# Latent attention on one core: groups of two heads and two query tiles, scores from row halves and row quarters, turned weights moved by two engines

## The chip, the cores and the metric

The kernel runs on one core of one Trainium2 chip. The metric is the device time of one execution in microseconds. The kernel before takes 4449.14 us in the median of three runs (4448.75 to 4455.67). All data is float32.

## The reference, cut to what matters

The program runs a window attention layer, a latent attention layer and then further layers (retention, stick-breaking, RWKV). Only the latent attention and the gate stage behind it are touched. Per head, with 1280 keys (256 of context, 1024 of the sequence) and 1024 queries:

```
s = (einsum("bqhd,bkhd->bhqk", qn, kn) + einsum("bqhd,bkd->bhqk", qr, kr)) * scale   # 64 deep, and 32 deep
p = softmax(s, axis=-1)
o = einsum("bhqk,bkhd->bqhd", p, v)
y = (o * silu(g)) @ w_out
```

There are 16 heads. The rope part `kr` is the same for all heads.

## The kernel before, in words

`latent_attention` (lines 1232 to 1427) works in units of one head and one query tile of 128 rows: 16 heads by 8 tiles make 128 units. Two neighbouring units of a head make a pair. Nope and rope rows of a head stand on 96 partitions of `qT` and `kT`, so that one float32 matmul computes a score chunk.

For a unit, PE makes the scores in three matmuls of 512, 512 and 256 columns into three banks (L1371). VectorE reads all 1280 at once into `s_sb`, scaled, with the row maximum (L1313), and negates the maximum (L1315). ScalarE takes the exponential in place, with the row sum (L1290). PE turns the ten 128 by 128 blocks of weights (L1389) into three banks; ScalarE moves eight of them to `pT` in two copies of 512 columns (L1301), VectorE two in a copy of 256 (L1329). For a pair of units PE multiplies the values (L1404): the two units go to the two column halves of the array, 64 columns each, so the result is a transposed `o`, which VectorE copies (L1323), PE turns back (L1376) and VectorE normalises into `o` (L1336).

The order on each engine is written out by hand. On PE it is, for unit u: scores of u + 1, one half of the values of an earlier pair, turning of u, and every second unit a turn back. A loop of six rounds runs over passes of two heads each, with a first and a last pass outside it.

SP loads a head with five transfers (L1268 to L1272) into one of two slots, and after the first two heads it prefetches (L161, L172) the gate weights `wg0` and `wg1` (2 MB each) and `wo` (4 MB) and two tiles of columns. `gate_and_project` (L753) then runs product with `wg`, silu, gating, turning and product with `wo`. Its window instance has only `wg0` prefetched and loads `wg1` and `wo` at its start; its latent instance before has all three prefetched.

Of the kernel before, what the change touches and what calls it, by code (L numbers as in the profile page):

```python
# [752 lines left out]
def gate_and_project(nc, core, name, o, tiles, weights, late, columns, gate_rows):  # L753


    with ExitStack() as mem:
# [13 lines left out]
        with nc.Block() as block:  # L770
# [30 lines left out]
            def _(dve):  # L801
                def gates(i):
                    dve.wait_ge(silu_made, i + 1)
                    dve.wait_ge(ogT_made, i)
                    dve.tensor_tensor(og[:, :], silu[:, :], o[:, tiles[i], :], ALU.mult).then_inc(og_made, 1)
# [426 lines left out]
def latent_attention(nc, core, q_dram, qr_dram, k_dram, kr_dram, v_dram, o, prefetch):  # L1232
# [5 lines left out]
    PASSES, UNITS, PAIRS = H // 2, 2 * QT, QT  # L1238
    FRONT_TILES, BACK_TILES = range(0, 4), range(4, 8)
    HALVES = [range(0, KT // 2), range(KT // 2, KT)]  # L1240
    with ExitStack() as mem:
        sb = lambda n, shape: mem.enter_context(nc.sbuf_tensor(f"{name}_{n}", shape, F32))
        qT, kT, v = sb("qT", [B_QK, 2, QT * P]), sb("kT", [B_QK, 2, K]), sb("v", [P, 2, KT, B_V])
        s_sb, pT, oT = sb("s", [P, 2, K]), sb("pT", [P, 3, K]), sb("oT", [P, 2, P])
        smax, total, inverse = sb("smax", [P, 2, 1]), sb("total", [P, 2, 2]), sb("inverse", [P, 2, 2])
        head_in = [nc.alloc_semaphore(f"{name}_head_in{s}") for s in range(2)]
        s_made, s_steps, p_made, pT_made, pT_act, pT_dve, o_made, oT_moved, inverse_made, back_read = (
            nc.alloc_semaphore(f"{name}_{n}") for n in (
                "s_made", "s_steps", "p_made", "pT_made", "pT_act", "pT_dve", "o_made", "oT_moved", "inverse_made", "back_read"))
        s_banks, pT_banks = core.banks(0, 3)[:, 0:K], [core.banks(3 + c) for c in range(3)]  # L1250
        tail_bank, back_bank = pT_banks[2][:, 0:2 * P], pT_banks[2][:, 2 * P:3 * P]
        o_bank = [core.banks(6 + n)[:, 0:P] for n in range(2)]

        def passes(eng, run):
            run(lambda per, k: k, True, False)
            with eng.Fori(0, PASSES - 2) as j:
                run(lambda per, k: j * per + (per + k), False, False)
            run(lambda per, k: (PASSES - 1) * per + k, False, True)

        pT_of = lambda u: (u // 2) % 2 if u % 2 == 0 else 2  # L1260
        with nc.Block() as block:

            @block.sync
            def _(sp):
                values_of = v_dram.rearrange("(t p) n -> p t n", p=P)

                def load(h, s):
                    sp.dma_start(qT[0:B_NOPE, s, :], q_dram[h]).then_inc(head_in[s], 16)  # L1268
                    sp.dma_start(qT[B_NOPE:B_QK, s, :], qr_dram[h]).then_inc(head_in[s], 16)
                    sp.dma_start(kT[0:B_NOPE, s, :], k_dram[h]).then_inc(head_in[s], 16)  # L1270
                    sp.dma_start(kT[B_NOPE:B_QK, s, :], kr_dram).then_inc(head_in[s], 16)
                    sp.dma_start(v[:, s, :, :], values_of[:, :, bass.ds(h * B_V, B_V)] if not isinstance(h, int) else values_of[:, :, h * B_V:(h + 1) * B_V]  # L1272
                                 ).then_inc(head_in[s], 16)

                load(0, 0)
                load(1, 1)
                prefetch(sp)
                with sp.Fori(0, PASSES - 1) as j:
                    for s in range(2):
                        hold(sp, o_made, j * PAIRS + (s + 1) * (PAIRS // 2))  # L1280
                        load(j * 2 + (s + 2), s)

            @block.scalar
            def _(act):
                one_table(act)

                def exp(count, u):
                    act.wait_ge(s_steps, count(UNITS * 2, u * 2 + 2))
# [1726 lines left out]
```

## Time and profile before

| what | before |
|---|---|
| time, median of three runs | 4449.14 us |
| time of the profiled execution | 4446.34 us |
| its span | 4444.3 us |
| mean granted TensorE clock | 0.969 |
| PE busy | 4115.8 us, 93% |
| PE weight loads busy | 2420.0 us, 54% |
| VectorE busy | 1506.5 us, 34% |
| ScalarE busy | 1223.9 us, 28% |
| score matmuls of the latent attention (L1371) | 300.9 us |
| its turning (L1389) | 168.9 us |
| its values (L1404) | 167.8 us |

How to read it: the span is what the profiler sees from first to last instruction. An engine's busy time joins overlapping instructions. A float32 matmul appears as two MATMUL records (two passes), a transpose as one. [...] "Idle before" is the time in which the engine had nothing in progress, with what ended it in brackets. The latent attention lies between 1229 and 1840 us of the span.

### The profile page before, as it was taken

How to read it: one execution, taken by the hardware profiler on the slowest of the kernel's cores; microseconds unless marked ns; L12 is line 12 of the kernel's file. 1: busy time of each engine (PE TensorE's matmuls, PEld its weight loads, DVE VectorE, ACT ScalarE, POOL GpSimd, SP SyncE). 2: the span in 40 equal slices, each digit the busy share in tenths (PEclk: the TensorE clock that was granted, in tenths of full speed). 3: DMA queues.
4: the chain of work that ended last, by engine and by line, in shares of the span. 5: the costliest groups of instructions: out<-in, count | busy, mean ns of one | idle time of the engine just before them, and what ended most of it. 6: DMA issues, size and time to landing. Idle time of an engine off the chain costs nothing. (4 is left out here: it accounts for less than half of the span.)

```text
span 4444.3 us, 69604 instructions
## 1 busy us (share of the span) xinstructions
PE 4115.8 (93%) x29154; PEld 2420.0 (54%) x29154; DVE 1506.5 (34%) x2878; ACT 1223.9 (28%) x2133; POOL 319.9 (7%) x143
## 2 busy tenths in 40 slices
PE   7999999989999999998999998998999968898798
PEld 1446864445466666543554455444444468888343
DVE  0335641122144544211331044012222266656111
ACT  0116750012245555301221045112222222211132
POOL 0000000000000000000000000000000037565000
PEclk9999999989999999999999999998999989999899
DMA  8200020042241111002002002005111121110300
GB/s 276 87 15 23 2 77 19 10 101 77 94 129 33 33 33 33 20 14 99 14 14 95 14 1 95 0 0 189 52 43 47 52 106 46 64 65 27 142 19 19
DMA packets 170633, 253.37 MB, mean 57 GB/s; under 512 B 79446, under 2 KB 97046, under 8 KB 170392
## 3 DMA queue, kind: packets, MB, share of 16 engines
q1 hardware_dynamic: 170398, 249.90, 16.9%
q8 instruction: 189, 3.10, 0.3%
q14 instruction: 46, 0.38, 0.0%
HBM read 187.27 MB, written 62.60 MB: 56 GB/s over the span
## 5 line engine op out<-in xcount | busy, mean ns | idle before, releaser
L237 PE MATMUL psum<-rp_w,rp_mixed 128*128 128x512 f32 x1024 | 448.2, 596 | 6.7 <-issue 3.6
L237 PEld LDWEIGHTS psum<-rp_w,rp_mixed 128*128 128x128 f32 x1024 | 194.3, 191 | 248.4 <-issue 242.2
L1371 PE MATMUL psum<-la_kT,la_qT 96*128 96x512 f32 (+1 forms) x768 | 300.9, 528 | 15.3 <-DMA la_v<-latent_v 13.0
L2323 POOL TENSOR_TENSOR rs_kk<-rs_k,rs_k_k 128x1024 f32<-128x1024 f32 x7 | 16.5, 2364 | 3711.7 <-DVE rs_k L2667 3589.0
L1313 DVE TENSOR_SCALAR_CACHE_REDUCE la_s<-psum 128x1280 f32<-128x1280 f32 x128 | 191.0, 1492 | 238.7 <-PE psum L1371 238.7
L237 PE MATMUL psum<-retention_w,even_hT 128*128 128x512 f32 x544 | 240.2, 603 | 7.8 <-PEq L112 6.3
L237 PE MATMUL psum<-output_wo,pg_oT 128*128 128x512 f32 x512 | 230.8, 610 | 11.5 <-DMA output_wo<-in_even_w_out_dram 5.4
L237 PE MATMUL psum<-output_wg,pg_xT 128*128 128x512 f32 x512 | 227.4, 602 | 7.3 <-ACT pg_xT L1954 7.3
L1301 ACT ACTIVATE la_pT<-psum 128x512 f32<-128x512 f32 x256 | 139.0, 595 | 289.7 <-PE psum L1389 289.7
L1371 PEld LDWEIGHTS psum<-la_kT,la_qT 96*128 96x128 f32 x768 | 137.1, 192 | 141.6 <-issue 128.2
L237 PEld LDWEIGHTS psum<-retention_w,even_hT 128*128 128x128 f32 x544 | 104.6, 194 | 137.3 <-issue 137.1
L1290 ACT ACTIVATE la_s<-la_s,la_smax 128x1280 f32<-128x1280 f32 x128 | 174.3, 1362 | 14.1 <-DVE la_smax L1315 14.1
L237 PEld LDWEIGHTS psum<-output_wo,pg_oT 128*128 128x128 f32 x512 | 99.9, 196 | 138.3 <-issue 125.6
L1389 PE MATMUL psum<-ident,la_s 128*128 128x128 f32 x1280 | 168.9, 279 | 0.5 <-ACT la_s L1290 0.5
L1404 PE MATMUL psum<-la_pT,la_v 128*64 128x128 f32 x2560 | 167.8, 278 | 0.6 <-ACT la_pT L1301 0.6
L237 PEld LDWEIGHTS psum<-output_wg,pg_xT 128*128 128x128 f32 x512 | 97.2, 193 | 128.4 <-issue 116.9
L1404 PEld LDWEIGHTS psum<-la_pT,la_v 128*64 128x64 f32 x2560 | 137.2, 136 | 42.4 <-issue 42.4
L2800 PE MATMUL psum<-rs_inverse,rs_Z 64*64 64x64 f32 x2560 | 153.9, 221 | 1.3 <-issue 0.2
L2162 ACT ACTIVATE x_rows<-psum 128x1024 f32<-128x1024 f32 x48 | 49.2, 1025 | 382.7 <-PE psum L237 369.4
L1389 PEld LDWEIGHTS psum<-ident,la_s 128*128 128x128 f32 x1280 | 138.9, 142 | 22.6 <-issue 21.6
L2798 PE MATMUL psum<-rs_Z,rs_inverse 64*64 64x64 f32 x2048 | 133.1, 222 | 16.2 <-DVE rs_Z L2625 15.9
L237 PE MATMUL psum<-window_o,window_hT 128*128 128x512 f32 x320 | 142.1, 598 | 2.6 <-DVE window_hT L458 2.6
(382 smaller groups left out, 6765.8 us busy)
## 6 DMA issues: line engine op xcount, KB each, us to landing
ada_slots<-in_ada_w_dram SPq DMA_DIRECT2D x12, 2048.0 KB, 19.4
rwkv_raw<-x_rows SPq DMA_DIRECT2D x48, 512.0 KB, 2.6
retention_w<-in_even_w_in_dram SPq DMA_DIRECT2D x8, 2048.0 KB, 12.2
rp_w<-in_odd_w_in_dram SPq DMA_DIRECT2D x4, 4096.0 KB, 29.8
output_wg<-in_ple_gate_dram SPq DMA_DIRECT2D x2, 4096.0 KB, 22.2
latent_v<-lp_v SPq DMA_DIRECT2D x10, 512.0 KB, 2.6
la_kT<-latent_kT SPq DMA_DIRECT2D x16, 320.0 KB, 4.5
la_v<-latent_v SPq DMA_DIRECT2D x16, 320.0 KB, 5.2
```

Of the source, the lines that this page charges most:

```text
L237: last = pe.matmul(out[:, c:c + w], left[:, k, :], right[:, k, c:c + w], start=(k == 0), stop=(k == kd - 1))
L1290: act.activation(s_sb[:, u % 2, :], s_sb[:, u % 2, :], ACT.Exp, bias=smax[:, u % 2, :], accum_out=total[:, p, u % 2:u % 2 + 1]).then_inc(p ...
L1301: act.activation(pT[:, pT_of(u), tiles[0] * P:(tiles[-1] + 1) * P], pT_banks[c], ACT.Copy).then_inc(pT_act, 1)
L1313: dve.tensor_scalar(s_sb[:, u % 2, :], s_banks, SCALE, NEG, ALU.mult, ALU.max, accum_out=smax[:, u % 2, :]).then_inc(s_steps, 1)
L1371: last = pe.matmul(s_banks[:, c:c + n], qT[:, s, q * P:(q + 1) * P], kT[:, s, c:c + n], start=True, stop=True)
L1389: last = pe.transpose(pT_banks[c][:, n * P:(n + 1) * P], s_sb[:, u % 2, t * P:(t + 1) * P], core.ident)
L1404: last = pe.matmul(o_bank[pair % 2][rows, :], v[:, s, t, :], pT[:, pT_of(2 * pair + n), t * P:(t + 1) * P], start=(t == 0), stop=(t == KT ...
L2162: act.activation(rows[:, m % 2, :], out_banks[m % 2], {G: ACT.Silu, W: ACT.Sigmoid, A: ACT.Sigmoid}.get(n, ACT.Copy)).then_inc(moved, 1)
L2323: eng.tensor_tensor(kk[:, :], k[s][:, :], k_k[:, :], ALU.mult).then_inc(q["kk_made"], 1)
L2798: pe.matmul(bank[chunk(c), n * C:(n + 1) * C], TT[chunk(c), h, :], Z[chunk(c), h, :], start=True, stop=True)
L2800: last = pe.matmul(bank[chunk(c), (GH + n) * C:(GH + n + 1) * C], Z[chunk(c), h, :], TT[chunk(c), h, :], start=True, stop=True)
```

## The change

`latent_attention` works in groups of two heads and two query tiles; 32 groups in all, in straight line instead of a loop. A group computes the scores of four (head, tile) rows of work, and each has a bank of its own. Scores come in three chunks of keys (512, 512, 256). In each chunk the nope parts are four matmuls on row halves of the array (head 0 on rows 0 to 63, head 1 on rows 64 to 127), then the rope parts are four matmuls on row quarters (32 rows each) that add to the same banks. The rope rows of queries and keys are loaded into tiles `qr` and `kr` of their own, the key one four times over.

VectorE reads each bank of each chunk on its own (12 reads for a group) with a partial maximum, and reduces the three to one. The 40 blocks of turned weights form ten fills of four blocks, in two banks in turn; ScalarE moves fills 0 to 3 and 5 to 8, VectorE fills 4 and 9. Values go, as before, to two column halves (the two tiles), head by head; the turned result goes back into the other part of the same bank.

SP loads a pair of heads with seven transfers. Only `wg0` is prefetched in the attention; `wg1` and `wo` are loaded by the gate stage at its start. The tile `o` has eight tiles instead of ten, hence `o_from`.

The diff, cut; lines taken out are left out:

```diff
+def gate_and_project(nc, core, name, o, o_from, tiles, weights, late, columns, gate_rows):
...
+                    dve.tensor_tensor(og[:, :], silu[:, :], o[:, tiles[i] - o_from, :], ALU.mult).then_inc(og_made, 1)
...
+    GROUPS_OF_PAIR, PAIRS = QT // 2, H // 2
+    G, FILLS, BLOCKS = PAIRS * (QT // 2), 4 * KT // 4, 4
+    CHUNKS = [slice(c, min(c + BANK, K)) for c in range(0, K, BANK)]
+    NC, LOADS = len(CHUNKS), 7
...
+        s_banks, pT_banks, o_banks = [core.banks(n) for n in range(4)], [core.banks(4 + n) for n in range(2)], [core.banks(6 + n) for n in range(2)]
+        slot = lambda g: (g // GROUPS_OF_PAIR) % 2
+        tile = lambda g: 2 * (g % GROUPS_OF_PAIR)
...
+                def load(p):
+                    slot = p % 2
+                    done = pair_in[slot]
+                    both = lambda t: t[2 * p:2 * p + 2].rearrange("h d t -> (h d) t")
+                    sp.dma_start(qT[:, slot, :], both(q_dram)).then_inc(done, 16)
+                    sp.dma_start(kT[:, slot, :], both(k_dram)).then_inc(done, 16)
+                    for h in range(2):
+                        for i in range(2):
+                            rows = slice(unit(h, i) * B_ROPE, (unit(h, i) + 1) * B_ROPE)
+                            sp.dma_start(qr[rows, slot, :], qr_dram[2 * p + h]).then_inc(done, 16)
+                    sp.dma_start(v[:, slot, :, :], values_of[:, :, 2 * p * B_V:(2 * p + 2) * B_V]).then_inc(done, 16)
+
+                load(0)
+                for n in range(4):
+                    sp.dma_start(kr[n * B_ROPE:(n + 1) * B_ROPE, :], kr_dram).then_inc(kr_in, 16)
+                load(1)
                 prefetch(sp)
...
+                for p in range(2, PAIRS):
+                    sp.wait_ge(o_made, 2 * GROUPS_OF_PAIR * (p - 1))
+                    load(p)
...
+                def move(g, f):
+                    h, at = f // (FILLS // 2), f % (FILLS // 2)
+                    act.wait_ge(pT_made, FILLS * g + f + 1)
+                    if g and at == 0:
+                        act.wait_ge(o_made, 2 * (g - 1) + h + 1)
+                    act.activation(pT[:, h, at * BANK:(at + 1) * BANK], pT_banks[f % 2], ACT.Copy).then_inc(pT_moved[f % 2], 1)
+
+                exp(0, 0)
+                exp(0, 1)
+                for g in range(G):
+                    move(g, 0)
+                    move(g, 1)
+                    exp(g, 2)
+                    move(g, 2)
+                    move(g, 3)
+                    exp(g, 3)
+                    for f in range(5, 9):
+                        move(g, f)
+                    if g + 1 < G:
+                        exp(g + 1, 0)
+                    if g + 1 < G:
+                        exp(g + 1, 1)
...
+                def read_scores(g, c, j):
+                    if c == 0 and g >= 2:
+                        dve.wait_ge(pT_made, FILLS * (g - 1))
+                    dve.wait_ge(s_made, NC * g + c + 1)
+                    cols = CHUNKS[c]
+                    dve.tensor_scalar(s_sb[:, g % 2, j, cols], s_banks[j][:, 0:cols.stop - cols.start], SCALE, NEG, ALU.mult, ALU.max,
+                                      accum_out=smax[:, g % 2, j, c:c + 1]).then_inc(s_read[j % 2], 1)
...
+                def evacuate(g, h):
+                    dve.wait_ge(o_made, 2 * g + h + 1)
+                    if g:
+                        dve.wait_ge(back_made, 2 * (g - 1) + h + 1)
+                    dve.tensor_copy(oT[:, h, :], o_banks[h][:, 0:P]).then_inc(oT_moved, 1)
...
+                for g in range(-1, G + 1):
+                    if g >= 1:
+                        evacuate(g - 1, 0)
+                    if g + 1 < G:
+                        for j in (0, 2, 1, 3):
+                            read_scores(g + 1, 0, j)
+                    if g >= 1:
+                        normalise(g - 1, 0)
+                    if g + 1 < G:
+                        for j in (0, 2, 1, 3):
+                            read_scores(g + 1, 1, j)
+                    if 0 <= g < G:
+                        move(g, 4)
+                    if g >= 1:
+                        evacuate(g - 1, 1)
+                    if g + 1 < G:
+                        for h in range(2):
+                            for i in range(2):
+                                read_scores(g + 1, 2, unit(h, i))
+                            maxima(g + 1, h)
+                    if g >= 1:
+                        normalise(g - 1, 1)
+                    if 0 <= g < G:
+                        move(g, 9)
...
+                def scores(g, c):
+                    s, cols, chunk = slot(g), CHUNKS[c], NC * g + c
+                    width = cols.stop - cols.start
+                    if c == 0 and g % GROUPS_OF_PAIR == 0:
+                        pe.wait_ge(pair_in[s], LOADS * 16 * (g // (2 * GROUPS_OF_PAIR) + 1))
+                    queries = lambda i: slice((tile(g) + i) * P, (tile(g) + i + 1) * P)
+                    for i in range(2):
+                        if chunk:
+                            pe.wait_ge(s_read[i], 2 * chunk)
+                        for h in range(2):
+                            rows = slice(h * B_NOPE, (h + 1) * B_NOPE)
+                            pe.matmul(s_banks[unit(h, i)][:, 0:width], qT[rows, s, queries(i)], kT[rows, s, cols], start=True, stop=False)
+                    if chunk == 0:
+                        pe.wait_ge(kr_in, 4 * 16)
+                    for h in range(2):
+                        for i in range(2):
+                            rows = slice(unit(h, i) * B_ROPE, (unit(h, i) + 1) * B_ROPE)
+                            last = pe.matmul(s_banks[unit(h, i)][:, 0:width], qr[rows, s, queries(i)], kr[rows, cols], start=False, stop=True)
                     last.then_inc(s_made, 1)
 
...
+                def fill(g, f):
+                    pe.wait_ge(p_made, 4 * g + (BLOCKS * f + BLOCKS - 1) // KT + 1)
+                    if FILLS * g + f >= 2:
+                        pe.wait_ge(pT_moved[f % 2], (FILLS * g + f) // 2)
+                    for n in range(BLOCKS):
+                        j, t = (BLOCKS * f + n) // KT, (BLOCKS * f + n) % KT
+                        last = pe.transpose(pT_banks[f % 2][:, n * P:(n + 1) * P], s_sb[:, g % 2, j, t * P:(t + 1) * P], core.ident)
+                    last.then_inc(pT_made, 1)
+
+                def values(g, h, half):
                     if half == 0:
...
+                        for n in range(2):
+                            pe.wait_ge(pT_moved[n], (FILLS * g + (h + 1) * FILLS // 2 + 1 - n) // 2)
+                        if g:
+                            pe.wait_ge(back_read, 2 * (g - 1) + h + 1)
                     for t in HALVES[half]:
...
+                        for i in range(2):
+                            last = pe.matmul(o_banks[h][i * B_V:(i + 1) * B_V, 0:P], v[:, slot(g), t, h * B_V:(h + 1) * B_V],
+                                             pT[:, h, i * K + t * P:i * K + (t + 1) * P], start=(t == 0), stop=(t == KT - 1))
                     if half:
                         last.then_inc(o_made, 1)
 
...
+                def turn_back(g, h):
+                    pe.wait_ge(oT_moved, 2 * g + h + 1)
+                    pe.transpose(o_banks[h][:, P:2 * P], oT[:, h, :], core.ident).then_inc(back_made, 1)
+
+                for g in range(-1, G + 1):
+                    ahead, here, behind = g + 1 < G, 0 <= g < G, g >= 1
+                    if ahead:
+                        scores(g + 1, 0)
+                    if behind:
+                        turn_back(g - 1, 0)
+                    if here:
+                        fill(g, 0)
+                        fill(g, 1)
+                    if behind:
+                        values(g - 1, 1, 0)
+                    if here:
+                        fill(g, 2)
+                        fill(g, 3)
+                    if ahead:
+                        scores(g + 1, 1)
+                    if here:
+                        fill(g, 4)
+                    if behind:
+                        values(g - 1, 1, 1)
+                    if here:
+                        fill(g, 5)
+                        fill(g, 6)
+                    if ahead:
+                        scores(g + 1, 2)
+                    if behind:
+                        turn_back(g - 1, 1)
+                    if here:
+                        values(g, 0, 0)
+                        fill(g, 7)
+                        fill(g, 8)
+                        values(g, 0, 1)
+                        fill(g, 9)
...
+            o = layer.enter_context(nc.sbuf_tensor("latent_o", [P, X_TILES, D], F32))
+            gate_halves = halves("wg", a["b_w_in"][0][:, B_LATENTS:])
+            first = Weights(nc, layer, "latent_first", {"wg0": gate_halves["wg0"]})
...
+                first.load(sp)
...
+            weights = Weights(nc, layer, "latent_gate", {"wg1": gate_halves["wg1"], "wo": ([P, KD, D], weight_blocks(a["b_w_out"][0]))})
+            weights.at["wg0"], weights.arrived["wg0"] = first.at["wg0"], first.arrived["wg0"]
             with stage(nc):
...
+                gate_and_project(nc, core, "lg", o, CTX_TILES, list(range(CTX_TILES, ALL_TILES)), weights, ("wg1", "wo"), columns, {0: rows[1, 0, 2 * D:]})
```

## Rows read from the trace of the kernel before

**Rows 1.** Busy time by engine, 1229 to 1841 us, with granted clock.
```profile
1229.00:1841.00 612.00, 606.67 (x4672) 416.34 (x4672) 298.18 (x704) 310.65 (x512) 0.00 (x0) 0.99 0.18 45
```

**Rows 2.** Who waited for whom, 1229 to 1840 us: total, times, longest.
```profile
ACT la_pT L1301 <- PE psum L1389: 289.7, 129, 4.0
```

**Rows 3.** Timeline of PE, two units: start, us, engine, line, form, count.
```profile
1501.47 1.31 PE L1404 MATMUL psum<-la_pT,la_v 128*64 128x128 f32 x20
1502.72 1.31 PE L1389 MATMUL psum<-ident,la_s 128*128 128x128 f32 x10
...
1503.98 2.31 PE L1371 MATMUL psum<-la_kT,la_qT 96*128 96x512 f32 x6
1506.22 1.31 PE L1404 MATMUL psum<-la_pT,la_v 128*64 128x128 f32 x20
...
1510.86 1.31 PE L1404 MATMUL psum<-la_pT,la_v 128*64 128x128 f32 x20
```

**Rows 4.** Timeline of PE at the start of the window layer's gate stage.
```profile
633.66 8.80 PE L237 MATMUL psum<-window_first_wg,window_hT 128*128 128x512 f32 x16 [1.46 <-PEq L112]
642.30 7.03 PE L237 MATMUL psum<-window_gate_wg,window_hT 128*128 128x512 f32 x16
649.17 7.03 PE L237 MATMUL psum<-window_first_wg,window_hT 128*128 128x512 f32 x16
```

**Rows 5.** Timeline of PE in the window attention.
```profile
501.33 1.36 PE L701 MATMUL psum<-window_kT,window_qT 64*128 64x256 f32 x12
502.62 1.09 PE L711 MATMUL psum<-ident,wa_s 128*128 128x128 f32 x8
503.55 0.38 PE L721 MATMUL psum<-ident,wa_s 128*128 128x128 f32 x2
503.77 0.27 PE L725 MATMUL psum<-ident,wa_oT 128*128 128x128 f32 x1
503.97 1.31 PE L738 MATMUL psum<-wa_pT,window_v 128*64 128x128 f32 x20
```

**Rows 6.** Timeline of PE in the scan stage: 64-row by 64-column quadrants.
```profile
3728.69 1.16 PE L2763 MATMUL psum<-rs_bT,rs_xT 64*64 64x64 f32 x64
```

**Rows 7.** Timeline of VectorE in the window attention: one 256-column read.
```profile
356.10 0.42 DVE L643 TENSOR_SCALAR_CACHE_REDUCE wa_s<-psum 128x256 f32<-128x256 f32 x1 [0.82 <-DVE wa_sink_scaled L628]
356.45 0.08 DVE L643 DVE_READ_ACCUMULATOR wa_s<-psum 128x1 f32 x1
```

**Rows 8.** Groups of VectorE by shape: busy, mean ns, idle before.
```profile
L1313 DVE TENSOR_SCALAR_CACHE_REDUCE la_s<-psum 128x1280 f32<-128x1280 f32 x128 | 191.0, 1492 | 238.7 <-PE psum L1371 238.7
...
L1695 DVE COPY stick_qT<-psum 128x512 f32<-128x512 f32 x8 | 5.5, 692 | 109.1 <-PE psum L1716 109.1
```

**Rows 9.** Timeline of all engines at the end of the latent attention.
```profile
1835.00 1.09 ACT L1301 ACTIVATE la_pT<-psum 128x512 f32<-128x512 f32 x2 [0.75 <-PE psum L1389]
...
1836.23 2.40 PE L1404 MATMUL psum<-la_pT,la_v 128*64 128x128 f32 x40 [0.61 <-ACT la_pT L1301]
...
1838.67 0.29 DVE L1323 COPY la_oT<-psum 128x128 f32<-128x128 f32 x1 [2.52 <-PE psum L1404]
...
1839.64 0.29 DVE L1336 TENSOR_TENSOR latent_o<-psum,la_inverse 128x128 f32<-128x128 f32 x1 [0.42 <-PE psum L1376]
```

**Rows 10.** The same timeline, earlier: one exponential of 1280 columns.
```profile
1828.16 1.36 ACT L1290 ACTIVATE la_s<-la_s,la_smax 128x1280 f32<-128x1280 f32 x1
...
1829.41 0.20 ACT L1290 ACTIVATION_READ_ACCUMULATOR la_s<-la_s,la_smax 128x1 f32 x1
```

**Rows 11.** Timeline of all engines at the start of the latent attention.
```profile
1220.34 0.53 SPq L1268 DMA_DIRECT2D la_qT<-latent_qT  x1
...
1229.15 4.63 PE L1371 MATMUL psum<-la_kT,la_qT 96*128 96x512 f32 x6 [13.05 <-DMA la_v<-latent_v]
...
1239.87 2.22 PE L1389 MATMUL psum<-ident,la_s 128*128 128x128 f32 x10
```

**Rows 12.** Busy time by engine, 1229 to 1240 us, with granted clock.
```profile
1229.00:1240.00 11.00, 9.16 (x13) 4.05 (x14) 1.65 (x3) 1.45 (x2) 0.00 (x0) 0.50 1.08 320
```

More of the change, by code:

```diff
@@ L1237, in latent_attention @@
     SCALE = B_QK ** -0.5
-    PASSES, UNITS, PAIRS = H // 2, 2 * QT, QT
-    FRONT_TILES, BACK_TILES = range(0, 4), range(4, 8)
+    GROUPS_OF_PAIR, PAIRS = QT // 2, H // 2
+    G, FILLS, BLOCKS = PAIRS * (QT // 2), 4 * KT // 4, 4
+    CHUNKS = [slice(c, min(c + BANK, K)) for c in range(0, K, BANK)]
+    NC, LOADS = len(CHUNKS), 7
     HALVES = [range(0, KT // 2), range(KT // 2, KT)]
+    unit = lambda h, i: 2 * h + i
     with ExitStack() as mem:
         sb = lambda n, shape: mem.enter_context(nc.sbuf_tensor(f"{name}_{n}", shape, F32))
[L1243 to L1247, printed above, removed]
-            nc.alloc_semaphore(f"{name}_{n}") for n in (
[L1249 to L1260, printed above, removed]
@@ L1361, in _ @@
             @block.tensor
             def _(pe):
-                def scores(count, u, first):
-                    s, q = (u % UNITS) // QT, u % QT
-                    if q == 0:
-                        pe.wait_ge(head_in[s], count(80, 80 * (u // UNITS + 1)))
-                    if not (first and u == 0):
-                        hold(pe, s_steps, count(UNITS * 2, (u - 1) * 2 + 1))
-                    for c in range(0, K, BANK):
-                        n = min(BANK, K - c)
-                        last = pe.matmul(s_banks[:, c:c + n], qT[:, s, q * P:(q + 1) * P], kT[:, s, c:c + n], start=True, stop=True)
-                    last.then_inc(s_made, 1)
@@ L1394, in values @@
-                def values(count, pair, half, first):
-                    s = (pair % PAIRS) * 2 // QT
+                def scores(g, c):
[16 more added lines that the diff above has]
+                            last = pe.matmul(s_banks[unit(h, i)][:, 0:width], qr[rows, s, queries(i)], kr[rows, cols], start=False, stop=True)
+                    last.then_inc(s_made, 1)
@@ L1401, in values @@
                     for t in HALVES[half]:
-                        for n in range(2):
-                            rows = slice(n * B_V, (n + 1) * B_V)
-                            last = pe.matmul(o_bank[pair % 2][rows, :], v[:, s, t, :], pT[:, pT_of(2 * pair + n), t * P:(t + 1) * P],
-                                             start=(t == 0), stop=(t == KT - 1))
+                        for i in range(2):
+                            last = pe.matmul(o_banks[h][i * B_V:(i + 1) * B_V, 0:P], v[:, slot(g), t, h * B_V:(h + 1) * B_V],
+                                             pT[:, h, i * K + t * P:i * K + (t + 1) * P], start=(t == 0), stop=(t == KT - 1))
@@ L1426, in _ @@
-                passes(pe, run)
+                def turn_back(g, h):
[34 more added lines that the diff above has]
+                        fill(g, 9)
@@ L2941, in prefetch @@
             def prefetch(sp):
-                weights.load(sp)
+                first.load(sp)
                 columns.load(sp, 0)
```

154 lines of the change are left out of this document (34 added, 120 removed).

## The prediction

> **What bounds the kernel now.** [...] The timeline of PE gives its stretches, each taken from its start to the start of the next: values 1.25 us for 20 passes, turning of weights 1.26 for 10 and the turn back, scores 2.24 for 6 passes; two units take 1510.86 - 1501.47 = 9.39, one 4.69, four 18.8 [rows 3].
>
> A float32 matmul is two passes, and a pass of 512 columns takes (649.17 - 642.30) / 16 = 0.43 us [rows 4]; in proportion 256 columns take 0.215, 128 take 0.107 (0.109 with the start of each). Scores: 4 x 0.43 + 2 x 0.215 = 2.15 of work and 0.09 of border. Values: 20 x 0.109 would be 2.18, but only 1.25 pass: the two column halves run two abreast, 1.09 of work and 0.15 of border. Four units: scores 8.60, values 4.36, turning 4.36, two turns back 0.22, sum 17.54; the rest of 18.8 is borders, 0.3 a unit.
>
> **The change on PE, per group** (two heads, two tiles: the work of four units, 32 groups). Turning, values and turns back stay 4.36 + 4.36 + 0.22. Scores are now two kinds. Nope rows, 64 deep: per 512-column chunk 8 passes. The window stage has such halves: 12 passes, eight of 256 and four of 128 columns, in 502.62 - 501.33 = 1.29 [rows 5]; singly they would need 8 x 0.215 + 4 x 0.107 = 2.15, so they run two abreast, 1.08 and 0.2 of border. So 4 x 0.43 = 1.72 for a 512 chunk, 0.86 for the 256 chunk, 4.30 a group. Rope rows, 32 deep in four quarters: no row shows this. The nearest is the scan stage's matmul on all four quadrants: 64 passes of 64 columns in 1.16, whose last record outlives its streaming by some 0.16 [rows 6]; singly they are 64 x 0.054 = 3.4, so they run 3.4 abreast or better. Ends: two abreast 4.30 a group, four abreast 2.15. I take 2.15, the quadrants being the nearer row. Work: 4.30 + 2.15 + 8.94 = 15.39, which is 2.15 less than before.
>
> Borders. The transposes between two tiled stretches in the window stage take 503.97 - 502.62 = 1.35 for 8 + 2 + 1 passes of 0.109, so 0.15 over [rows 5]. A stretch of half rows has 0.2, of half columns 0.15, before returning to whole [rows 3, 5]. After the change PE passes through, per group, 3 stretches of halves, 3 of quarters (not shown in the trace: between 0 and 0.2 each; I take 0.2, as for halves), 4 of values and 7 of whole-array work (turn back with fills 0, 1; fills 2, 3; fill 4; fills 5, 6; turn back; fills 7, 8; fill 9). That is 3 x 0.2 + 3 x 0.2 + 4 x 0.15 + 7 x 0.15 = 2.85, where four units had 1.2. Without a wait a group takes 15.39 + 2.85 = 18.24: four fifths of the gain is spent on borders.
>
> [...]
>
> **The new wait.** There are two banks for fills, and fill 6 needs the one that VectorE empties as fill 4. VectorE has queued ahead of that move four reads of the score chunk just made. A 256-column read takes 0.35 to its accumulator read, plus 0.08 and a start, 0.45 [rows 7]; a 1280-column one 1.49, with the same additions some 1.53 [rows 8]; in between, 0.715 for 512. VectorE starts about 0.2 after the last pass has streamed (0.04 after the shown end) and PE 0.11 to 0.14 after a move ends [rows 9]. Counted from the end of the scores: 0.2 + 4 x 0.715 + 0.69 (a 512 copy [rows 8]) + 0.11 = 3.86. PE meanwhile has fill 4, values and fill 5: (0.15 + 0.44) + (0.15 + 1.09) + (0.15 + 0.44) = 2.42. So fill 6 waits 1.44, behind it the last score chunk and all that follows; nothing else on PE is queued to fill it. The other waits close: after the first chunk PE has four fills and half of the values, over 3 us, against 2.9 of reads. ScalarE needs per group 8 moves at 0.5 and 4 exponentials at about 1.46, 10 us of 19 [rows 9, 10]; VectorE 8 x 0.715 + 4 x 0.45 + 2 x 0.69 and about 1.8 of small ones, 10.7. Neither bounds. Group: 18.24 + 1.44 = 19.7, against 18.8, so +0.9.
>
> **Ends of the stage.** [...] After, scores and reads of the first group alternate. The first chunk's scores are 0.2 + 1.72 + 0.2 + 0.86 = 2.98; the second chunk may start 0.2 + 2 x 0.715 + 0.16 later (its first bank pair read), at 4.8 from the start; its second half waits for the other pair, so the third starts 5.1 on, at 9.9; the next group's first chunk, queued ahead of the first fill, starts at 14.5 and takes 2.98: first fill at 17.4. [...] The first period lacks the earlier group's values and turns, so 31 periods are 607. The last group has from its first fill: fills 0 to 6 with the old values 6.4, turn back and values and fills 7 to 9 to 10.6, VectorE's copy of fill 9 to 11.5, evacuation and turn back, values 2.2 and a second evacuation, turn back and normalising: 15.5. Sum 21 + 607 + 15.5 = 643.5. Before: 1839.64 - 1229.15 = 610.5 [rows 9, 11]. So +33. The first load is 2.36 MB in seven transfers, not 1.18 in five; from 1220.34 to 1229.15 the old one took 8.8 with the second head's sharing the queue [rows 11], so I add 3 (0 to 8). Later pair loads have three groups, 55 us, to land.
>
> Two of three gate weights move from the attention to the start of the gate stage. I cost that at nothing: the window's gate stage has this very order, its first 16 passes take 642.30 - 633.66 = 8.64, and the product with the late half follows with no idle time shown [rows 4]. The cover is that first product; without it up to those 8.6 would stand open. The larger output weight has three more such products before it. Less prefetching in the attention frees nothing that PE waits for. Unrolling the loop, the smaller output tile and the maxima in two steps: nothing on PE.
>
> Total: 33 + 3 = +36 on the profiled execution's 4446.3, which is 3 under the median of 4449.1: 4482. I keep the sum against the profiled execution's time.
>
> **Rivals.**
> (a) The halves-to-quarters border is free: 0.2 x 3 x 32 = 19 less, 4463. For it: both are row tilings; against: every measured change of tiling costs.
> (b) Quarters are slower than four abreast since four score banks are written at once: a third slower, near three abreast, is +0.7 x 32 = +22, 4504. The trace shows two banks at once at no loss [rows 5], four tiles on quadrants near full. [...]
> (c) Quarters run two abreast: +2.15 x 32 = +69, 4551. Speaks for it that each matmul's two passes must follow each other; against, [rows 6].
> (d) On the other side, faster: PE loads the next tiles ahead and the borders around the scores vanish, those into halves, into quarters and out: (0.2 + 0.2 + 0.15) x 3 x 32 = 53 less, 4429. It decides for faster once a chunk pays under 0.11 of these 0.55, since 4482 - 4440 = 42 = 0.44 x 96. The window stage shows two of the three borders in full, hence little chance.
> (e) Small terms all at their low ends (free inner border, 0.15 into halves, reads of 0.69, no load delay): the group takes 18.8, as now: 4451.
>
> **How the numbers follow.** Forecast 0.51, (a) 0.14, (b) 0.13, (c) 0.07, (d) 0.06, (e) 0.09. Range 4450 to 4525: it leaves out (c), (d) and a little of the others. About 0.2% (9 us) is what a measurement of this kernel can tell from no change. Faster by more: 0.06, (d). Within: (e) and the low tail of (a), 0.12. Slower: 0.82.
>
> **What would show it.** Per group 19.7 us on PE; fill 6 waiting some 1.4 us for VectorE's copy, 45 us in all; score chunks of 512 columns taking 1.9 for halves and 1.05 for quarters, start to start; VectorE reads near 0.7. Wrong if quarters start later than a few ns after each other, if fill 6 finds its bank free, or if another wait shows more than 0.3 us a group.

## The result and the profile after the change

The changed kernel takes 4485.03 us, the kernel before 4456.78 in runs beside it (medians of seven runs each): the ratio is 1.0065 with a 95% interval of 1.0051 to 1.0080. It is slower by some 28 us, as forecast (4482, range 4450 to 4525). The profiled execution took 4485.03 us.

The page of the changed kernel (span 4483.3 us), its engines; VectorE has gained work, PE has hardly more:

```profile
PE 4117.7 (92%) x29922; PEld 2391.6 (53%) x29922; DVE 1517.2 (34%) x3326; ACT 1223.8 (27%) x2133; POOL 320.9 (7%) x143
```

The attention stage in one window (columns: length, then busy us and instructions of PE, PE's weight loads, VectorE, ScalarE, GpSimd, the granted clock, DMA share, GB/s), to hold against [rows 1]:

```profile
1232.00:1868.00 636.00, 595.85 (x5440) 378.49 (x5440) 307.19 (x1152) 310.48 (x512) 0.00 (x0) 0.99 0.11 33
```

PE computes for 595.85 us where [rows 1] had 606.67, so the row tiling does give something. But PE now stands still for 40 of 636 us, where it stood still for 5 of 612. One group of two heads and two query tiles on PE, to hold against the two units of [rows 3] (start, us, line, operation, times; in brackets the idle time before it):

```profile
1500.81 1.99 PE L1396 MATMUL psum<-la_kT,la_qT 64*128 64x512 f32 x8
1502.73 1.14 PE L1402 MATMUL psum<-la_kr,la_qr 32*128 32x512 f32 x8
1503.80 0.33 PE L1429 MATMUL psum<-ident,la_oT 128*128 128x128 f32 x1
1503.96 1.04 PE L1411 MATMUL psum<-ident,la_s 128*128 128x128 f32 x8
1504.93 1.31 PE L1422 MATMUL psum<-la_pT,la_v 128*64 128x128 f32 x20
1506.17 1.10 PE L1411 MATMUL psum<-ident,la_s 128*128 128x128 f32 x8
1507.20 1.99 PE L1396 MATMUL psum<-la_kT,la_qT 64*128 64x512 f32 x8
1509.12 1.14 PE L1402 MATMUL psum<-la_kr,la_qr 32*128 32x512 f32 x8
1510.19 0.66 PE L1411 MATMUL psum<-ident,la_s 128*128 128x128 f32 x4
1510.77 1.31 PE L1422 MATMUL psum<-la_pT,la_v 128*64 128x128 f32 x20
1512.02 0.66 PE L1411 MATMUL psum<-ident,la_s 128*128 128x128 f32 x4
1513.61 0.63 PE L1411 MATMUL psum<-ident,la_s 128*128 128x128 f32 x4 [0.93 <-DVE la_pT L1340]
1514.16 1.14 PE L1396 MATMUL psum<-la_kT,la_qT 64*128 64x256 f32 x8
1515.23 0.71 PE L1402 MATMUL psum<-la_kr,la_qr 32*128 32x256 f32 x8
1515.87 0.33 PE L1429 MATMUL psum<-ident,la_oT 128*128 128x128 f32 x1
1516.13 1.31 PE L1422 MATMUL psum<-la_pT,la_v 128*64 128x128 f32 x20
1517.38 1.09 PE L1411 MATMUL psum<-ident,la_s 128*128 128x128 f32 x8
1518.40 1.31 PE L1422 MATMUL psum<-la_pT,la_v 128*64 128x128 f32 x20
1519.64 0.66 PE L1411 MATMUL psum<-ident,la_s 128*128 128x128 f32 x4
1520.23 1.99 PE L1396 MATMUL psum<-la_kT,la_qT 64*128 64x512 f32 x8
```

A group takes 1520.23 - 1500.81 = 19.42 us, four units took 18.77. The ten fills of a group are the lines of L1411, four passes each and two fills in a line of eight; fill 6, at 1513.61, is the one stretch with idle time before it. The group's twelve nope matmuls are 24 records and its 40 blocks 40, so a float32 matmul shows as two records and a transpose as one. Records overlap: the eight at 1500.81 last 1.99 together, and the next kind starts 1.92 after their start, so all stretches are taken from start to start. The waits (us in all, times, longest) say the same for all groups; ScalarE, as in [rows 2], still waits for PE most of the time:

```profile
PE psum L1411 <- DVE la_pT L1340: 30.3, 31, 2.3
ACT la_pT L1301 <- PE psum L1411: 303.2, 127, 4.5
```

What VectorE does just then (all engines' timeline, its lines alone): four reads of the scores, the first at 1510.33 (the last two are shown), and only then the copy of fill 4 that fill 6 waits for:

```profile
1511.55 0.69 DVE L1326 TENSOR_SCALAR_CACHE_REDUCE la_s<-psum 128x512 f32<-128x512 f32 x1
...
1512.16 0.69 DVE L1326 TENSOR_SCALAR_CACHE_REDUCE la_s<-psum 128x512 f32<-128x512 f32 x1
...
1512.77 0.69 DVE L1340 COPY la_pT<-psum 128x512 f32<-128x512 f32 x1
```

The start of the stage, to hold against [rows 11]:

```profile
1221.73 0.33 SPq L1270 DMA_DIRECT2D la_qT<-latent_qT  x1
...
1232.31 3.79 PE L1396 MATMUL psum<-la_kT,la_qT 64*128 64x512 f32 x8 [14.82 <-DMA la_v<-latent_v]
...
1238.82 2.35 PE L1396 MATMUL psum<-la_kT,la_qT 64*128 64x512 f32 x8 [1.44 <-DVE la_s L1326]
...
1247.94 1.99 PE L1396 MATMUL psum<-la_kT,la_qT 64*128 64x512 f32 x8 [1.70 <-DVE la_s L1326]
...
1250.93 1.09 PE L1411 MATMUL psum<-ident,la_s 128*128 128x128 f32 x8
```

and the gate product at its end, to hold against the end in [rows 9] and, for the order of the weights, [rows 4]:

```profile
1868.95 7.11 PE L237 MATMUL psum<-latent_first_wg,latent_hT 128*128 128x512 f32 x16 [2.19 <-PEq L112]
1876.59 7.13 PE L237 MATMUL psum<-latent_gate_wg,latent_hT 128*128 128x512 f32 x16 [0.54 <-DMA latent_gate_wg<-in_b_w_in_dram]
```

From the first load of the attention to the first matmul of the gate product the stage takes 1868.95 - 1221.73 = 647.2 us; the kernel before takes 621.3. The other 12.8 of the 38.7 between the two profiled executions lie elsewhere. 1.4 are there before the stage begins (its first load is issued at 1221.73, not 1220.34). The largest part, 9.1, is in the scan stage, whose code is the same in both. Before, and after:

```profile
3605.40:4103.30 497.90, 439.08 (x12892) 413.17 (x12886) 325.64 (x519) 99.70 (x159) 296.92 (x130) 0.97 0.15 50
```
```profile
3635.60:4142.60 507.00, 446.70 (x12890) 419.85 (x12888) 327.62 (x519) 99.46 (x159) 298.03 (x130) 0.96 0.15 49
```

That stage varies between executions of kernels that are the same there: 495.7 in experiment e7b_order, 515.6 in e6_full_rows_act4, at a granted clock of 0.97 and 0.95. So the single executions differ by 38.7 us, the medians by 28, the stage by 25.9. For the reasons I go by the period of a group (the same stretch of the order, one group later) and by the stage.

### The profile page after: what moved, and what is told of

It is laid out like the page before. It is cut to its first block and busy times, and to the rows that moved or that the text cites. A ratio compares the mean times of both kernels' runs of the same rounds, so it can differ in the third digit from the quotient of the medians.

```text
span 4483.3 us, 70281 instructions
## 1 busy us (share of the span) xinstructions
PE 4117.7 (92%) x29922; PEld 2391.6 (53%) x29922; DVE 1517.2 (34%) x3326; ACT 1223.8 (27%) x2133; POOL 320.9 (7%) x143
## 5 line engine op out<-in xcount | busy, mean ns | idle before, releaser
L1326 DVE TENSOR_SCALAR_CACHE_REDUCE la_s<-psum 128x512 f32<-128x512 f32 (+1 forms) x384 | 210.5, 598 | 281.7 <-PE psum L1402 281.7
L1411 PE MATMUL psum<-ident,la_s 128*128 128x128 f32 x1280 | 186.0, 280 | 31.0 <-DVE la_pT L1340 30.3
L1396 PE MATMUL psum<-la_kT,la_qT 64*128 64x512 f32 (+1 forms) x768 | 166.8, 552 | 20.0 <-DMA la_v<-latent_v 14.8
L1411 PEld LDWEIGHTS psum<-ident,la_s 128*128 128x128 f32 x1280 | 137.6, 141 | 83.9 <-issue 81.5
L1293 ACT ACTIVATE la_s<-la_s,la_negm 128x1280 f32<-128x1280 f32 x128 | 174.2, 1366 | 24.6 <-DVE la_negm L1335 24.6
L237 PE MATMUL psum<-window_gate_wo,wg_ogT 128*128 128x512 f32 x320 | 139.9, 595 | 1.4 <-DVE wg_y_gated L811 1.4
## 6 DMA issues: line engine op xcount, KB each, us to landing
retention_w<-in_even_w_in_dram SPq DMA_DIRECT2D x8, 2048.0 KB, 12.4
```

The lines of the kernel that those rows point to most:

```text
L237: last = pe.matmul(out[:, c:c + w], left[:, k, :], right[:, k, c:c + w], start=(k == 0), stop=(k == kd - 1))
L1293: act.activation(s_sb[:, g % 2, j, :], s_sb[:, g % 2, j, :], ACT.Exp, bias=negm[:, g % 2, j:j + 1], accum_out=total[:, g % 2, j:j + 1]).th ...
L1326: dve.tensor_scalar(s_sb[:, g % 2, j, cols], s_banks[j][:, 0:cols.stop - cols.start], SCALE, NEG, ALU.mult, ALU.max, accum_out=smax[:, g % ...
L1396: pe.matmul(s_banks[unit(h, i)][:, 0:width], qT[rows, s, queries(i)], kT[rows, s, cols], start=True, stop=False)
L1411: last = pe.transpose(pT_banks[f % 2][:, n * P:(n + 1) * P], s_sb[:, g % 2, j, t * P:(t + 1) * P], core.ident)
```

## The experiments

Theory: the row tiling saves PE somewhat more than its borders cost, and the move of fill 4 behind VectorE's reads takes more than that back. Rivals: the quarters are slower than four abreast (b, c), the borders around the scores vanish (d), or the loss is in the group scheme itself: its start, its end, its late weights. Period and stage are measured in each kernel as above.

| kernel | period of a group | stage | time |
|---|---|---|---|
| before | 18.77 (four units) | 621.3 | 4456.78 |
| the change | 19.42 | 647.2 | 4485.03 |
| e1_act4 | 18.30 | 610.4 | 4443.31 |
| e2_move_first | 18.89 | 630.8 | 4458.60 |
| e3_no_rope | 16.61 | 559.6 | 4394.34 |
| e4_two_quarters | 21.54 | 718.3 | 4560.98 |
| e5_full_rows | 20.01 | 670.7 | 4516.57 |
| e6_full_rows_act4 | 18.77 | 628.3 | 4466.07 |
| e7b_order | 17.84 | 595.2 | 4431.06 |
| e8_before_late | 18.77 | 621.3 | 4451.50 |

e1, e6 and e7b are medians of several rounds beside the kernel before; e2 to e5 and e8 are one run each.

**e1_act4: ScalarE moves fill 4 as well, VectorE only fill 9.**

```
                 # ScalarE
-                    for f in range(5, 9):
+                    for f in range(4, 9):
...
                 # VectorE, behind the reads of the second chunk
-                    if 0 <= g < G:
-                        move(g, 4)
```

> The changed kernel with fill 4 moved by ScalarE instead of VectorE; nothing else. Theory (fill 6 waits because VectorE reads four score banks before it copies fill 4): the 1.0 us wait before fill 6 goes, a group takes 18.4 instead of 19.42 us, the kernel loses about 32 us against the changed one and comes out near the kernel before, 4 to 8 us under it. Rival (the wait only moves: ScalarE gets late with the copy or with the exponentials of the next group): 19.0 or more a group and a new wait on ScalarE shown before a fill. Rival (VectorE as a whole has too little time): little changes, since it sheds only one copy of 0.69 us.

4443.31 us against 4458.25 for the kernel before: 0.9967, interval 0.9952 to 0.9982. The period falls from 19.42 to 18.30 and the stage from 647.2 to 610.4, 11 less than before the change. On PE fills 5 and 6 have become one stretch without idle time, and between 1255 and 1800 us the list of PE's waits has a single line left:

```profile
1512.35 1.09 PE L1409 MATMUL psum<-ident,la_s 128*128 128x128 f32 x8
```
```profile
PE psum L1409 <- ACT la_pT L1301: 0.3, 1, 0.3
```

The move is worth 1.12 us a group, more than the 0.93 of idle time shown: a record runs some 0.16 past the point where a successor can start (a turn back's record at 1515.48 lasts 0.27 in e6, and its successor starts 0.11 after it), and 0.93 + 0.16 leaves 0.03. Taking this one move back turns a kernel that is 0.65% slower into one that is 0.33% faster. I had expected a period of 18.4 and 4 to 8 us under the kernel before; it is 18.30 and 15 under (11 in the stage), so the gain was larger than forecast.

**e2_move_first: VectorE keeps fill 4, but copies it ahead of the four reads.**

```
+                    if 0 <= g < G:
+                        move(g, 4)
                     if g + 1 < G:
                         for j in (0, 2, 1, 3):
                             read_scores(g + 1, 1, j)
-                    if 0 <= g < G:
-                        move(g, 4)
```

> The changed kernel with VectorE's copy of fill 4 put ahead of its four reads of the second score chunk; the same instructions in another order. Theory: fill 6 finds its bank free, but the reads start some 0.75 us later and the second half of the third chunk's scores waits about 0.5 us for them; a group takes 18.9 instead of 19.42 us. If VectorE's amount of work were what counts and not its order, a group would stay at 19.4.

Period 18.89, stage 630.8. The wait for the copy is gone (0.4 us in all between 1255 and 1800, against 27.5 in the changed kernel), so it was the place in the queue and not the engine that made it. What is late next are the reads behind the copy; the third score chunk now finds the second pair of its banks unread:

```profile
1503.39 0.70 PE L1396 MATMUL psum<-la_kT,la_qT 64*128 64x256 f32 x4
1504.42 0.70 PE L1396 MATMUL psum<-la_kT,la_qT 64*128 64x256 f32 x4 [0.32 <-DVE la_s L1326]
1505.05 0.71 PE L1402 MATMUL psum<-la_kr,la_qr 32*128 32x256 f32 x8
```

The waits for it between 1255 and 1800 us:

```profile
PE psum L1396 <- DVE la_s L1326: 10.1, 30, 0.5
```

The chunk's halves take 1505.05 - 1503.39 = 1.66 where they take 1.06 in e1, and that is the 0.59 by which the period is above e1's. So about half of the loss stays, in the other of the two places tried for VectorE's copy.

**e3_no_rope: the rope quarters are left out.** The 32-row matmuls and their wait are removed, the nope matmuls close the sum.

```
-        pe.matmul(s_banks[unit(h, i)][:, 0:width], qT[rows, s, queries(i)], kT[rows, s, cols], start=True, stop=False)
...
-        pe.wait_ge(kr_in, 4 * 16)
...
-        last = pe.matmul(s_banks[unit(h, i)][:, 0:width], qr[rows, s, queries(i)], kr[rows, cols], start=False, stop=True)
+        last = pe.matmul(s_banks[unit(h, i)][:, 0:width], qT[rows, s, queries(i)], kT[rows, s, cols], start=True, stop=True)
```

> The changed kernel without the rope part of the scores (the 12 quarter matmuls of a group are left out). Theory (quarters four abreast and a border of 0.2 us of their own): 2 x 0.86 + 0.43 of work and 3 x 0.2 of border go, 2.75 us a group, 19.42 to 16.7, with the wait of fill 6 unchanged at 1.0. Rival (the border between halves and quarters is free, only the return to the whole array is paid, which stays): 2.15 less, 17.3.

Period 16.61, so the quarters cost 2.81 a group, close to the 2.15 + 3 x 0.2 = 2.75 of the prediction. Rival (a), a free border from halves to quarters, asked for 2.15. The wait for fill 4 stays (29.7 us in all, 0.91 in most groups), so it doesn't hang on the quarters. And the halves alone show their border:

```profile
1500.36 1.99 PE L1396 MATMUL psum<-la_kT,la_qT 64*128 64x512 f32 x8
1502.27 0.66 PE L1405 MATMUL psum<-ident,la_s 128*128 128x128 f32 x4
```

8 passes two abreast are 4 x 0.43 = 1.72, and from start to start they take 1.91, so some 0.2 goes to the border.

**e4_two_quarters: both query tiles of a head on the same quarter, so two quarters at work instead of four.**

```
-                            rows = slice(unit(h, i) * B_ROPE, (unit(h, i) + 1) * B_ROPE)
+                            rows = slice(unit(h, 0) * B_ROPE, (unit(h, 0) + 1) * B_ROPE)
```

> The changed kernel with both query tiles of a head on the same row quarter (the rope rows are stored four times over, so the result is the same): quarter 0 for head 0, quarter 2 for head 1, banks as before. Theory (passes run abreast only on different row quarters): two abreast, 2.15 us more a group, 21.5 to 21.6 instead of 19.42. Rival (passes run abreast because they write different banks): 19.4.

Period 21.54, 2.12 more; two abreast instead of four was priced at 2.15. A chunk's quarters take from start to start what the halves take:

```profile
1509.48 1.99 PE L1396 MATMUL psum<-la_kT,la_qT 64*128 64x512 f32 x8
1511.40 1.99 PE L1402 MATMUL psum<-la_kr,la_qr 32*128 32x512 f32 x8
1513.32 0.33 PE L1429 MATMUL psum<-ident,la_oT 128*128 128x128 f32 x1
```

In the changed kernel the same step takes 1.07 = 2 x 0.43 + 0.21: four abreast in full. The width says the same without e4: its 256-column chunk takes 1515.87 - 1515.23 = 0.64, so 256 columns more cost 0.43 where 8 passes singly would need 8 x 0.215 = 1.72, and the 0.21 is there at both widths. That ends (b) and (c).

**e5_full_rows: nope and rope stacked to 96 rows, one matmul for each bank and chunk, no row tiling at all.** The groups, the order and the move of fill 4 stay. A pair needs nine loads, not seven.

```
-        qT, kT, v = sb("qT", [P, 2, QT * P]), sb("kT", [P, 2, K]), sb("v", [P, 2, KT, 2 * B_V])
-        qr, kr = sb("qr", [P, 2, QT * P]), sb("kr", [P, K])
+        qT, kT, v = sb("qT", [B_QK, 2, 2, QT * P]), sb("kT", [B_QK, 2, 2, K]), sb("v", [P, 2, KT, 2 * B_V])
...
+        last = pe.matmul(s_banks[unit(h, i)][:, 0:width], qT[:, s, h, queries(i)], kT[:, s, h, cols], start=True, stop=True)
```

> The changed kernel with its scores as before the change: nope and rope rows of a head on 96 partitions, one matmul per bank and chunk, no row tiling; groups, banks, reads and moves as in the changed kernel. Theory (row tiling saves 2.15 us of passes and pays 1.65 of borders, and the wait of fill 6 has nothing to do with it): work 17.54 + 4 value stretches with both borders 1.2 + wait 1.1 = 19.85 to 20.0 us a group, against 19.42. Rival (the borders eat the whole gain): 19.4. Rival (row tiling brings its 2.15 us in full, and groups and separate reads cost more than thought): above 21.

Period 20.01, 0.59 above the change and at the upper end of the 19.85 to 20.0 expected. One chunk takes 8 x 0.43 = 3.44 from start to start, with no border, and the wait for fill 4 is there too, a little longer:

```profile
1501.04 3.60 PE L1390 MATMUL psum<-la_kT,la_qT 96*128 96x512 f32 x8
1504.48 0.60 PE L1399 MATMUL psum<-ident,la_s 128*128 128x128 f32 x4
...
1507.96 0.63 PE L1399 MATMUL psum<-ident,la_s 128*128 128x128 f32 x4 [1.05 <-DVE la_pT L1335]
```

**e6_full_rows_act4: e5 with e1's edit**, so the group scheme without the row tiling and without the move.

> As the kernel without row tiling, and fill 4 moved by ScalarE, so without the wait. Theory: 18.75 to 18.85 us a group, which is what four units take before the change (18.77), and 0.45 to 0.5 more than the same kernel with row tiling (18.30). In time about 15 us above that one, within 0.2% of the kernel before, a little above it for the slower start of the stage. If it stays at 18.3, row tiling earns nothing.

Period 1518.73 - 1499.96 = 18.77, exactly that of four units of the kernel before; 4466.07 us against 4460.96, ratio 1.0015, interval 1.0004 to 1.0025.

```profile
1499.96 3.60 PE L1388 MATMUL psum<-la_kT,la_qT 96*128 96x512 f32 x8
...
1518.73 3.60 PE L1388 MATMUL psum<-la_kT,la_qT 96*128 96x512 f32 x8
```

With e1 this splits the change's 0.65 a group into -0.47 from the row tiling (18.30 - 18.77) and +1.12 from the move (19.42 - 18.30). The parts depend a little on the order in which they are taken: with e5 the move comes first and costs 1.24 (20.01 - 18.77), and the row tiling then brings 0.59 (19.42 - 20.01), since the wait is 0.12 longer without it. The grouping itself costs PE nothing a group; the 7 us by which this kernel's stage is longer than before the change lie at its two ends, 3.6 of them between the first load and the first score (12.37 against 8.81).

**e8_before_late: the kernel before with only the first half of the gate's weights loaded ahead.**

```
-                **halves("wg", a["b_w_in"][0][:, B_LATENTS:]), "wo": ([P, KD, D], weight_blocks(a["b_w_out"][0]))})
...
+            first = Weights(nc, layer, "latent_first", {"wg0": gate_halves["wg0"]})
...
-                gate_and_project(nc, core, "lg", o, list(range(CTX_TILES, ALL_TILES)), weights, (), columns, {0: rows[1, 0, 2 * D:]})
+                gate_and_project(nc, core, "lg", o, list(range(CTX_TILES, ALL_TILES)), weights, ("wg1", "wo"), columns, {0: rows[1, 0, 2 * D:]})
```

> The kernel before with one part of the change: only the first half of the gate weights is prefetched in the attention, the other half and the output weights are loaded by the gate stage at its start. Theory: 0 to 0.6 us in the gate stage, a wait before its second product; the attention's units stay at 4.69 us. Rival (prefetching 8 MB slowed the attention): its units or its start get faster.

The stage stays at 621.3 and the late half costs a fifth of a microsecond. The gate product starts at 1843.30, and its second 16 passes, the first with the late half, wait 0.18:

```profile
1852.29 7.13 PE L237 MATMUL psum<-latent_gate_wg,latent_hT 128*128 128x512 f32 x16 [0.18 <-DMA latent_gate_wg<-in_b_w_in_dram]
```

In the changed kernel that wait is 0.54. Less prefetching didn't speed the attention up either: 18.77 and 621.3 both ways.

**e7b_order: can the borders be saved too?** From e1, with PE's order rewritten so that whole-array work comes in fewer, longer stretches (S: scores, F: fills, V: values, T: turn back): S0, F0 F1, V, S1, F2 F3, V, F4 T F5, S2, T F6 F7, V V, F8 F9. That is 14 stretches a group, not 17. VectorE moves fills 7 and 9, behind the reads of the third chunk and the second head's normalising; ScalarE moves the other eight.

```
                 # PE, one group
+                    if ahead:
+                        scores(g + 1, 1)
...
-                    if ahead:
-                        scores(g + 1, 1)
+                    if behind:
+                        values(g - 1, 1, 1)
...
+                        fill(g, 6)
+                        fill(g, 7)
                         values(g, 0, 0)
-                        fill(g, 7)
+                        values(g, 0, 1)
                         fill(g, 8)
-                        values(g, 0, 1)
                         fill(g, 9)
```

> The changed kernel with other orders on the engines: PE has 14 stretches in a group instead of 17 (scores 0; fills 0, 1; values; scores 1; fills 2, 3; values; fills 4, 5 with both turns back around scores 2; fills 6, 7; both halves of the next values together; fills 8, 9); ScalarE moves fills 0 to 6 and 8, VectorE 7 and 9, so two of ten as in the changed kernel. Theory (what costs are borders of 0.15 to 0.2 us and the one wait): no wait on PE, 17.8 to 17.9 us a group, 0.45 less than with fill 4 on ScalarE alone (18.30), about 14 us less in time, 0.6 to 0.7% under the kernel before. Rival (shorter gaps between PE's stretches uncover another wait, on ScalarE's copies or VectorE's reads): 18.3 or more, with that wait in the trace.

4431.06 us against 4460.96: 0.9945, interval 0.9932 to 0.9959. The period is 1520.30 - 1502.46 = 17.84, 0.46 less than e1, which is about three borders of 0.15. The time is 0.55% under the kernel before, where 0.6 to 0.7% was expected; the stage is 15.1 us shorter than e1's, where 14 were. Two of values' stretches have become one:

```profile
1502.46 1.99 PE L1395 MATMUL psum<-la_kT,la_qT 64*128 64x512 f32 x8
...
1511.69 2.40 PE L1421 MATMUL psum<-la_pT,la_v 128*64 128x128 f32 x40
1514.03 1.09 PE L1410 MATMUL psum<-ident,la_s 128*128 128x128 f32 x8
...
1520.30 1.13 PE L1395 MATMUL psum<-la_kT,la_qT 64*128 64x512 f32 x4
```

40 passes of values take 2.34 with one border where twice 20 took 2.49. PE is busy 574.62 of 584 us in its attention window at a granted clock of 1.00. This kernel is faster than the kernel before, and than the change, which is 0.65% slower than the kernel before.

## Why the prediction was right, and where its terms were off

Before the change the stage hung on PE, idle for 5 of 612 us [rows 1], with ScalarE waiting for it [rows 2]. The prediction's direction and its two causes stood: the row tiling pays for little more than its borders, and the move of fill 4 costs more than what remains. Term by term:

- **Work and borders of the scores: right.** Halves 1.92 a chunk of 512 columns, quarters 1.07, values 1.24 for 20 passes, 0.15 back to the whole array (the turn back at 1515.87 takes 0.26 to the next start instead of 0.11). Without the wait I had 18.24 a group, e1 shows 18.30. The sign of being wrong, quarters that start later than a few ns after each other, is not there: the window 1502.70 to 1502.75 already has the first four of a chunk's eight records, and the other four start at 1503.26. What the rows show more closely: a 512-column chunk gains 3.44 - 1.92 - 1.07 = 0.45 and pays 0.15 to come back, so 0.30; a 256-column chunk takes 1.07 + 0.64 = 1.71 where whole rows would take 8 x 0.215 = 1.72, and so loses the 0.15. Two of the first and one of the second are 0.45, and e6 less e1 is 0.47. Whole rows for the short chunk alone would by this save 0.15 a group; that wasn't tried.
- **The wait: right in place, too large.** It was to cost 1.44 a group, 45 us in all. By e1 it costs 1.12; the idle time shown is 0.93 in this group and 30.3 us in all. The term that was mis-sized is the read of 512 columns, put at 0.715 with its accumulator read and a start: the reads follow at 0.61 (1511.55 to 1512.16), shorter than one of them lasts, so neither the accumulator read nor the start adds anything. Four times 0.105 is 0.42: from the start of fill 4 to that of fill 6 pass 3.42 and not 3.86. Some 0.1 runs the other way, since PE itself is sooner ready for fill 6: I had given fills 4, values and 5 a border each, but fills 5 and 6 are of one shape and take 1.03 together in e1, not twice 0.59. The interpolation between [rows 7] and [rows 8] took additions for serial that overlap. No other wait on PE comes to 0.3 a group.
- **The start: too slow.** The first fill came 18.6 after the first score, not 21. The 21 is an estimate of mine: 17.4 by steps, and the rest for half of PE's 7.6 at a granted clock of 0.50 as in [rows 12]. No run shows that share. Only the first eight passes, the halves of the first chunk, ran at 0.50: they take 3.72 from start to start where later ones take 1.92, and the granted clock is 0.50 in them and 1.00 from 1237.4 on (the windows below are of the first and the second chunk's halves). In the kernel before it was 0.50 for 11 us [rows 12]. The second chunk's halves still take 2.28, at a granted clock of 1.00: their second four passes start 1.22 after the first four, at 1240.04, just after the last of VectorE's four reads (1239.29, lasting 0.69), so I read it as a wait for banks that the overlapping records hide. The waits of the scores for VectorE's reads, 1.44, 1.43 and 1.70, are there as described.

```profile
1232.30:1236.00 3.70, 3.69 (x8) 1.19 (x8) 0.00 (x0) 0.00 (x0) 0.00 (x0) 0.50 1.00 305
1238.80:1241.10 2.30, 2.19 (x9) 0.61 (x9) 1.18 (x4) 0.00 (x0) 0.00 (x0) 1.00 1.19 253
```

- **The first load: +1.8, not +3.** 1232.31 - 1221.73 = 10.58 against 8.81. e5 and e6, with nine loads, need 12.4.
- **The late weights: nearly nothing, as said.** 0.54 of wait, and it hangs on how fast the product ahead of it runs: the first 16 passes took 7.11 in the changed kernel, at a granted clock of 1.00, and 8.80 in e8, at 0.80, with a wait of 0.18; e3, e4, e6 and e7b, with 8.6 to 8.8, have none. The first 64 passes of the gate product took 28.35 (1897.30 - 1868.95), less than the 29.24 of the kernel before. Why the clock there differs between kernels wasn't tested.
- **The sum.** From the first score to the gate product: 636.6 against 612.5 before, +24.1 where I had +33. Of the 9 that are missing 2.4 are the start and 6.6 the later part, with the wait too long by some 0.3 a group as its main term (19.42 a group and not 19.7; over 31 groups this is 8.7, so other terms behind the first fill were 2 too short). With the load's 1.8 the stage makes +25.9 against +36. The median of all runs says +28. That 4485 is so near to 4482 is partly luck: the forecast of +36 was too large by 8 against the medians and by 10 in the stage, and the median of the kernel before had moved up by 8, from 4449 to 4457.

**The rivals.** (a) fell by e3: the halves take 1.91 there before whole-array work and 1.92 in the changed kernel before the quarters, so that border is as dear as one to the whole array. (b) and (c) fell by e4 and the 1.07. The step from two to four quarters is a full factor of two, 1.92 - 0.20 = 1.72 in e4 against 1.07 - 0.21 = 0.86 in the changed kernel; with its border a chunk of quarters takes 3.44 / 1.07 = 3.2 times less than the 8 passes of e5 one after another. The two passes of a matmul do follow each other, as (c) has it, the second four records of a chunk starting 0.53 after the first four (1502.73 and 1503.26), but four matmuls run abreast all the same. The third by which (b) has quarters slower was an assumption, and no run shows it: it would make the 0.86 a 1.15. (d) fell, each border is paid. (e) was right about the reads, which at 0.61 are below even its 0.69, wrong in its borders, and half right about the load (+1.8, between its nothing and my 3).

**What stays open.** The stage's ends: the stage grew by 25.9, 32 groups account for 20.8, the load for 1.8, and the 3.3 that remain I put down to the start and the end. They were read from the timeline and not tested by a kernel of their own; e1 and e7b leave 2.5 and 1.6 by the same sum. Why the scan stage varies by up to 20 us between executions isn't explained here.

## What to carry to other kernels

Price a tiling by its stretches, not by its rows: here each change of shape cost 0.15 to 0.20 us, the row tiling kept 0.47 of the 2.15 us that it saved in passes, a chunk of 256 columns gained nothing, and putting equal shapes together (17 stretches to 14) was worth as much as the tiling itself. When work is handed to an engine with plenty of idle time, ask what stands ahead of it in that engine's queue and which buffer waits for it: one copy behind four reads cost 1.12 us a group and turned the sign of the change, and the same copy ahead of the reads still cost half of it. And before calling a short wait small, multiply it by the groups.

## What the runs showed of the hardware that I had not expected

- VectorE's reads of the score banks, 512 columns wide with a row maximum, follow each other at 0.61 us in the changed kernel (1511.55, 1512.16) though each lasts 0.69; the accumulator read of the one at 1511.55, 0.08 long, starts at 1512.16 together with the next read.
- Four 32-row quarters with 512 columns each ran fully four abreast in the changed kernel: 8 passes took 0.86 and a border of 0.21, in four banks, each of the four float32 matmuls with two records; with two quarters in e4 the same passes took 1.72 and 0.20.
- The border from halves to quarters cost as much as the one from halves to the whole array: 8 passes that are 1.72 of work took 1.92 before the one (the changed kernel) and 1.91 before the other (e3).
- Idle time shown on PE understated what the wait for fill 4 cost: 0.93 shown in the changed kernel against 1.12 in the period (19.42 - 18.30 in e1); the overlap of records, 0.27 - 0.11 = 0.16 in e6, is most of the difference.
